# ScalarE's work in the attention stage in another order, with the block loads of queries and keys on ScalarE's queue

## The reference

```python
# A: neighbourhood attention, 4 heads of 64, a window of 8 x 16 tokens, and 512 context keys
s_lat = einsum('bhrqd,bhrikd->bhrqik', qg, kg) + bias      # -inf outside the window's columns
s_ctx = einsum('bhrqd,bhcd->bhrqc', qg, ck)
p = softmax(concatenate([s_lat, s_ctx], -1))
o = einsum('bhrqik,bhrikd->bhrqd', p_lat, vg) + einsum('bhrqc,bhcd->bhrqd', p_ctx, cv)
# D: chunked gated linear attention, both directions, a chunk of 64 tokens
o_intra = where(causal, q_dec @ k_inv, 0) @ v
state = decay * state + k_end @ v;  o_inter = q_dec @ state_at_start
```

## Time and profile before

| | us |
|---|---|
| median of 3 runs (lowest, highest) | 2887.41 (2885.74, 2889.26) |
| the profiled execution, its own time | 2884.65 |
| its span in the profile | 2882.9 |
| TensorE busy in the span | 2549.0 (88%) |
| ScalarE busy in the span | 971.1 (34%) |
| the attention stage: first scores to last scan output | 1660.3 to 2300.0 |

### The profile page before, as it was taken

One profiled execution on the slowest core, in us unless ns is written; L12 is line 12 of the kernel. 1 busy time (PEld: TensorE's weight loads), 2 busy tenths in 40 slices (PEclk: granted clock), 3 DMA queues, 4 the chain that ended last, 5 costly groups with the idle time before them and its releaser, 6 DMA issues. The chain is left out here.

```text
span 2882.9 us, 53072 instructions
## 1 busy us (share of the span) xinstructions
PE 2549.0 (88%) x18772; PEld 2050.2 (71%) x18772; DVE 1261.2 (44%) x2644; ACT 971.1 (34%) x1991; POOL 795.0 (28%) x1273
## 2 busy tenths in 40 slices
PE   3899999999999689999999577888888754899999
PEld 1688888888888578888888456666666622688887
DVE  2534434343443243333333145665666511666665
ACT  2444444444444332222222134544545411211110
POOL 2223333332333200000000134434444300444442
PEclk8999999999999889999999789999999978899999
DMA  7433333333333342222222488876777599666664
GB/s 286 139 108 113 116 121 102 117 120 106 115 115 104 112 168 100 95 95 95 95 95 88 108 175 182 180 163 157 167 164 167 122 282 245 219 205 206 206 205 143
DMA packets 286657, 425.19 MB, mean 147 GB/s; under 512 B 45045, under 2 KB 203029, under 8 KB 282795
## 3 DMA queue, kind: packets, MB, share of 16 engines
q1 hardware_dynamic: 273132, 389.25, 47.3%
q10 hardware_dynamic: 12831, 32.85, 3.3%
q0 software_dynamic: 544, 1.09, 0.2%
HBM read 288.74 MB, written 134.34 MB: 147 GB/s over the span
## 5 line engine op out<-in xcount | busy, mean ns | idle before, releaser
L258 PE MATMUL p_ps_m<-p_w_hi,p_h_hi 128*128 128x512 f32 x1904 | 771.1, 405 | 20.3 <-DVE p_h_lo L768 19.5
L259 PE MATMUL p_ps_m<-p_w_lo,p_h_hi 128*128 128x512 f32 x1904 | 750.7, 394 | 0.0
L260 PE MATMUL p_ps_m<-p_w_hi,p_h_lo 128*128 128x512 f32 x1904 | 749.1, 393 | 0.0
L258 PEld LDWEIGHTS p_ps_m<-p_w_hi,p_h_hi 128*128 128x128 f32 x1904 | 359.2, 189 | 99.5 <-issue 20.3
L260 PEld LDWEIGHTS p_ps_m<-p_w_hi,p_h_lo 128*128 128x128 f32 x1904 | 358.8, 188 | 80.5
L259 PEld LDWEIGHTS p_ps_m<-p_w_lo,p_h_hi 128*128 128x128 f32 x1904 | 359.5, 189 | 72.6
L258 PE MATMUL o_ps_y<-o_w_hi,o_y_hi 128*128 128x512 f32 x544 | 218.4, 401 | 9.7 <-DVE o_y_lo L1744 9.7
L259 PE MATMUL o_ps_y<-o_w_lo,o_y_hi 128*128 128x512 f32 x544 | 218.2, 401 | 0.0
L260 PE MATMUL o_ps_y<-o_w_hi,o_y_lo 128*128 128x512 f32 x544 | 214.5, 394 | 0.0
L1267 PE MATMUL a_ps_o<-a_v_win,a_p_t 128*64 128x64 f32 x2112 | 94.2, 230 | 100.8 <-DMA a_kv<-s_kv 39.8
L1267 PEld LDWEIGHTS a_ps_o<-a_v_win,a_p_t 128*64 128x64 f32 x2112 | 77.1, 140 | 138.6 <-issue 89.9
(11 more groups left out here) (202 smaller groups left out, 4469.7 us busy)
## 6 DMA issues: line engine op xcount, KB each, us to landing
p_xr<-in_x_sample SPq DMA_DIRECT2D x64, 512.0 KB, 3.9
p_xt<-in_x_sample_t SPq DMA_DIRECT2D x64, 512.0 KB, 4.6
a_scan<-s_scan SPq DMA_DIRECT2D x68, 258.0 KB, 5.6
s_scan<-p_w_raw SPq DMA_DIRECT2D x136, 128.0 KB, 2.4
a_kv<-s_kv SPq DMA_DIRECT2D x68, 256.0 KB, 6.3
a_v_win<-s_p SPq DMA_DIRECT2D x132, 128.0 KB
o_x<-in_x_sample SPq DMA_DIRECT2D x32, 512.0 KB, 4.9
out_y_sample<-o_y ACTq DMA_DIRECT2D x32, 512.0 KB, 4.4
```

The source lines that it names most:

```text
L258: pe.matmul(out, left_hi(k), right_hi(k), start=(k == 0), stop=False)
L259: pe.matmul(out, left_hi(k), right_lo(k), start=False, stop=False)
L260: last = pe.matmul(out, left_lo(k), right_hi(k), start=False, stop=(k == K8 - 1))
```

## The change

ScalarE's order within a unit is new. Before it was: copy of `v`, `copy_scan` at head 0, both exponentials of `v+2`, `scale_out` of `v`. Now it is: copy of `v`, the context exponential of `v+1`, `scale_out` of `v-1`, `copy_scan` at head 0, the window exponential of `v+2`. The loads of the next block's queries and keys leave SyncE's program and stand at the end of ScalarE's: three of queries at `c = 0`, head 0, three at `c = 0`, head 1, three of keys at `c = 1`, head 0, and three at `c = 2`, head 0. The very first block is still loaded by SyncE. TensorE, VectorE and GpSimd keep their programs, with all their waits.

```diff
@@ block.sync @@
-                if c < 3 and b is not None:
-                    after = next_tile(i + 3 - c, jb, b, 3, kb)
-                    if c == 0:
-                        if not isinstance(jb, int) or jb:
-                            sp.wait_ge(s_done, jb * 16)
-                            sp.wait_ge(q_set, jb * 8)
-                        load_queries(after[1], after[2], after[4])
-                    else:
-                        load_keys(after[1], after[2], after[4], (c - 1,))
@@ block.scalar @@
+        def unit_before(tile, h):
+            i, jb, b, c, kb = tile
+            return (tile, h - 1) if h else ((i - 1, jb, b, (c + 3) % 4, kb), NH - 1)
+        def unit_after(tile, h):
+            return (tile, h + 1) if h + 1 < NH else (next_tile(*tile), 0)
...
-            def exps(tile, h):
+            def exp_window(tile, h):
                 i, jb, b, c, kb = tile
                 p = h % 2
                 act.wait_ge(max_done, 4 * i + h + 1)
+                if b is not None:
+                    act.activation(s_sb[p][:, 0:N_WIN], s_sb[p][:, 0:N_WIN], ACT.Exp, bias=neg_m[:, p:p + 1], accum_out=sums[:, p, 0:1])
+            def exp_context(tile, h):
+                i, jb, b, c, kb = tile
+                p = h % 2
                 if b is None:
...
                 else:
-                    act.activation(s_sb[p][:, 0:N_WIN], s_sb[p][:, 0:N_WIN], ACT.Exp, bias=neg_m[:, p:p + 1], accum_out=sums[:, p, 0:1])
                     act.activation(s_sb[p][:, WIN_P:], ps_c[p][:, :], ACT.Exp, bias=neg_m[:, p:p + 1],
                                    accum_out=sums[:, p, 1:2]).then_inc(exp_done, 1)
...
                         act.activation(p_t[h % 2][:, WIN_P:], ps_t[1][:, :], ACT.Copy).then_inc(t1_sb, 1)
+                    next_one, next_h = unit_after(tile, h)
+                    if next_one:
+                        exp_context(next_one, next_h)
+                    if not isinstance(i, int) or v:
+                        scale_out(*unit_before(tile, h))
                     if h == 0 and (not isinstance(i, int) or i):
                         copy_scan(i - 1, 1 - c % 2)
                     ahead_tile, ahead_h = units_ahead(tile, h)
                     if ahead_tile:
-                        exps(ahead_tile, ahead_h)
-                    scale_out(tile, h)
+                        exp_window(ahead_tile, ahead_h)
+                    if b is not None and (c == 0 and h < 2 or c in (1, 2) and h == 0):
+                        after = next_tile(i + 3 - c, jb, b, 3, kb)
+                        if c == 0 and h == 0 and (not isinstance(jb, int) or jb):
+                            act.wait_ge(s_done, jb * 16)
+                            act.wait_ge(q_set, jb * 8)
+                        if c == 0:
+                            load_queries(after[1], after[2], after[4], (h,))
+                        else:
+                            load_keys(after[1], after[2], after[4], (c - 1,))
+            scale_out((LAST_STEP, BLOCKS, None, 1, 0), NH - 1)
```

More of the change, by code:

```diff
@@ L978, in load_keys, with load_queries @@
                     sp.dma_start(low_keys[kb][:, h::2, 0:n].bitcast(F32), io["qk_lo"][2:4, half, bass.ds(tok, n)].rearrange("p k t -> k p t")).then_inc(k_in[kb], 16)
-            def load_queries(jb, b, kb):
+            def load_queries(jb, b, kb, parts):
                 tok, n = (N_GRID, N_PROMPT) if b is None else (b * BQ, BQ)
-                for h in range(2):
+                for h in parts:
                     half = slice(h * HD, h * HD + HD)
@@ L1018, in load_bias @@
                                  io["btab"][e, :, :, first - r + WIN_H - 1:first - r + 2 * WIN_H - 1, :].rearrange("h q r x -> q h (r x)")).then_inc(bias_in[e], 16)
-            load_queries(0, BLOCKS - 1, 0)
+            load_queries(0, BLOCKS - 1, 0, range(2))
             load_keys(0, BLOCKS - 1, 0, range(2))
@@ L1038, in _ @@
                           *(n for d in DIRS for n in (tile_of(d, ni) * (HD * SCAN_W * 4), tile_of(d, ni) * (P * 2 * W_GRP * 4), tile_of(d, i - 1) * (P * W_GRP * 4))))
-                    if c == 0:
-                        ahead(sp, jb * 16, jb * 8, (b + 1) * (BQ * 4))
-                    elif c < 3:
-                        ahead(sp, key_at(b + 1) * (GRID_W * 4))
                 if nxt:
@@ L1166, in _, with load_keys, load_queries @@
             act.activation(ck_dup[:, :, :], ck_f[:, :, :], ACT.Copy).then_inc(ck_hi_done, 1)
-            def exps(tile, h):
+            def load_keys(jb, b, kb, parts):
+                tok, n = (N_GRID, N_PROMPT) if b is None else (key_at(b) * GRID_W, BK)
+                for h in parts:
+                    half = slice(h * HD, h * HD + HD)
+                    high = io["qk_hi"][2:4, half, bass.ds(tok, n)].rearrange("p k t -> k p t")
+                    for z in range(2):
+                        act.dma_start(k_dup[kb][z * HD:z * HD + HD, h::2, 0:n].bitcast(F32), high).then_inc(k_in[kb], 16)
+                    act.dma_start(low_keys[kb][:, h::2, 0:n].bitcast(F32), io["qk_lo"][2:4, half, bass.ds(tok, n)].rearrange("p k t -> k p t")).then_inc(k_in[kb], 16)
+            def load_queries(jb, b, kb, parts):
+                tok, n = (N_GRID, N_PROMPT) if b is None else (b * BQ, BQ)
+                for h in parts:
+                    half = slice(h * HD, h * HD + HD)
+                    high = io["qk_hi"][0:2, half, bass.ds(tok, n)].rearrange("p k t -> k p t")
+                    act.dma_start(q_blk[kb][0:HD, h::2, 0:n].bitcast(F32), high).then_inc(q_in[kb], 16)
+                    act.dma_start(low_q[kb][:, h::2, 0:n].bitcast(F32), high).then_inc(q_in[kb], 16)
+                    act.dma_start(q_blk[kb][HD:P, h::2, 0:n].bitcast(F32), io["qk_lo"][0:2, half, bass.ds(tok, n)].rearrange("p k t -> k p t")).then_inc(q_in[kb], 16)
+            def exp_window(tile, h):
                 i, jb, b, c, kb = tile
@@ L1196, in _ @@
             first = (0, 0, BLOCKS - 1, 0, 0)
-            exps(first, 0)
-            exps(first, 1)
+            exp_window(first, 0)
+            exp_context(first, 0)
+            exp_window(first, 1)
             for tile in query_tiles(act):
```

## The result

The changed kernel takes 2978.36 us (median of 4 runs, 2972.07 to 2982.49), against 2886.57 us (4 runs) before: a ratio of 1.0313, 95% interval 1.0295 to 1.0330. It is slower by 92 us, where 2923.5 was forecast with a range up to 2958. The profiled execution took 2979.53 us.

A forecast was written before the change was run, and what follows sets the result against it. TensorE was taken to bound most attention steps, with waits for `a_kv` and ScalarE's copy. 2884.65 + 48 (order) + 10 (loads on ScalarE) - 22 (SyncE) = 2920.7, plus 2.8 to the runs' median: 2923.5 us, range 2900 to 2958.

The forecast's parts named there:

- The direction: Whole kernel: slower 0.86, within 0.2% (5.8 us) of no change 0.05, faster 0.09.
- From `turn` to `values`: TensorE, attention tiles: 3.53 us instead of 2.67 at head 0, 2.74 at heads 1 to 3.
- The sum of +48: ScalarE's new order in the attention stage: +1.50 us per tile over 32 grid tiles, bounds 45 to 67.
- the 0.86 of that head: Head 0: `values` comes 3.53 us after `turn` instead of 2.67, since `copy_scan` now follows the later `scale_out`.
- The loads on ScalarE, +10: Block-load issues on ScalarE: 2.4 us at head 0, 8 at `c = 0`, head 1; between 3 and 35.
- rival 2: ScalarE's block-load issues take 1.2 us each, costing 49 in place of 10: 2962 us, chance 0.11.
- The late copy at `c = 0`, head 2: ScalarE: the load set at head 1 delays this copy by 0.96 us, 8 us together over 8 sets.
- What SyncE wins, -22: SyncE without block loads: TensorE's waits for `a_kv` shrink, 27 us won and 5 lost again.
- 3 to 5 us to spare: Next tile's scan data: landed at 18 to 20 us after `turn` of head 0, needed by TensorE at 22.7.
- Rival 1: Key transfers exceed the spare time, so the `a_kv` waits stay: 2946 to 2978 us, chance 0.17.
- Rivals 3 and 4: Rival 3: new order under 0.5 per tile, 2864, chance 0.08; rival 4: order at 0.5, about 2887, chance 0.06.

The follow-up runs named there:

- the fastest version of all: Against the kernel before: `scale_out` ahead of the copy, `copy_scan` right behind it, SyncE's stores behind its loads, block loads still on SyncE; 2871.13 us, ratio 0.9941.
- the run with the stores behind: Against the changed kernel: SyncE issues the loads of tile `i+1` first and stores tile `i-1` behind them; 2912.82 us, ratio 1.0093.

## Where the prediction was right and where it failed

**The direction was right** (slower, 0.86), the time was not: 2978.4 against 2923.5, 20 us above the range.

**From `turn` to `values`: right to 0.04 in the loop's tiles.** Forecast 3.53 at head 0 and 2.74 at heads 1 to 3, measured 3.53 and 2.70 to 2.71; undisturbed tiles 19.2 forecast, 18.9 to 19.1 measured where no issue stands in the way. The largest wait for ScalarE is the one for `scale_out`, but not the largest at `values`: that is the one for `a_kv` (79.0 against 73.6). **The sum of +48 was too large**: the order alone costs 31.6, with an interval of 24 to 37. A tile that waits for `a_kv` at head 0 doesn't pay the 0.86 of that head (11 tiles, some 9 us). The other 7 can be noise for the most part: the two profiled executions differ by 38.5 (2923.16 less 2884.65), which with the 9 makes the 48. That the cause is the place of `scale_out` behind the context exponential is shown for heads 1 to 3, where nothing else was moved when the cost went; at head 0 `copy_scan` was moved with it.

**The loads on ScalarE, +10: nearly nothing.** An issue takes 0.61, as forecast, so rival 2 (1.2 each) is out. But a set's first issue starts 0.13 to 0.30 after the window exponential has *started* (1908.77 and 1908.64), not behind its end, and so a set is over some 0.5 sooner than I had it. The late copy at `c = 0`, head 2, was forecast for all 8 blocks with 0.96; `values` is late there in 4 of the 8, by 0.35 to 0.60, 1.9 us in all. At head 1 there is a set in which one issue takes 1.93. The copy starts 0.12 after the last issue of that set ends, and `values` comes 0.6 late:

```profile
1953.71 1.93 ACTq L1179 DMA_DIRECT2D a_k_low<-s_qk_hi  x1
...
1955.73 0.61 ACTq L1180 DMA_DIRECT2D a_q_blk<-s_qk_lo  x1
1956.46 0.60 ACT L1225 ACTIVATE a_p_t<-a_ps_t 128x512 f32<-128x512 f32 x1 [3.01 <-PE a_ps_t L1280]
```

With the bytes taken away and the issues left, the time is 2915.3, not above that of the order alone. The issues cost more than a few us only where they were put at heads 2 and 3.

**What SyncE wins, -22: this is the step that failed, with its sign.** I counted SyncE's own time as what was short and took it as freed: values issued in 2.98 to 4.57, landing 6.3 later, 3 to 5 us to spare. The trace of before already speaks against it. In each of the 32 grid tiles SyncE waits for `scale_out` before its stores, 168.6 us in all. In the tile at 1907.78 the last load of queries is out at 1922.75, and the stores can start only at 1925.68. The block loads stood in time that SyncE had to wait anyway, so that taking them away moves no store and no load of a tile forward; in the changed kernel SyncE waits 294.1 us.

What the move did was the opposite of a gain: the waits for `a_kv` grew by 39.2 us, and their landing rose from 6.3 to 8.4. SyncE's issues did not get quicker either. The values' slow issue was there before (its rows from 1680 us on add up to some 143 us, twelve of them 5.4 to 8.0, more than the 4.57 that I took as the worst) and is there after (148); new is the slow load of scan data (53 us before, 87 after, twelve rows of 2.98 to 4.03). Slow issues of values alone need not cost: the fastest version of all has the most, some 171 us. Before, the block loads stood last on the common queue, behind what the next tile needs, and that order was worth more than the 4 us of issuing. Alone, the move costs 38.9.

**Rival 1** (the transfers' waits stay, 2946 to 2978, chance 0.17) was the right mechanism: three loads of keys or queries don't fit into the time to spare. That the measured time is at its very end is in part luck. The rival's sum has 58 us for the order and the issues, of which 31.6 and a few were measured, and it had the bytes' part too small: the waits not only stayed but doubled, and after the long ones the clock was lower. I had held against it that the keys are issued some 4 us ahead of the scan data; the runs with the loads two heads later show that this is what does the harm. The Trainium skill's rule ("DMA: Bandwidth & Descriptors", sections "Issuing engines are not separate DMA queues" and "Queues, rings and completion order") had stood against my gain: transfers of different engines share the same DMA engines, and a second issuing engine saves only issuing time. The runs agree: 2978.4 with the bytes, 2915.3 without, the issues the same.

**Rivals 3 and 4** need a new order at 0.5 per tile or less: it costs about 1 (31.6 over 32 tiles). The version with `scale_out` in front of the copy shows that such an order exists, and then 2885.7 comes out.

**The whole loss.** Of 91.8 us, 31.6 are the order, 38.9 the loads, and 21.3 more come only with both; by the intervals of the three runs this last figure is uncertain by some 12. Part of it is the clock. Matmul time per recorded matmul in the loop is 222.47/3688 = 60.3 ns; before it was 251.49/4320 = 58.2, with the loads alone 237.59/4035 = 58.9 and with the order alone 236.29/4084 = 57.9. At some 270 matmuls a tile (3688 in 13.6 tiles) and 32 tiles that is an estimated 18 us against before, 6 with the loads alone and -3 with the order alone, so some 15 of the 21. The rest would be that a later section and slower transfers come out of the same spare time; the run with the stores behind, which gives back 65.5, fits that, but the two were not separated. Open, too, is how the doubled waits divide in the changed kernel between slower issuing of scan data (as at 1916) and slower landing, which alone does it in the run with the loads alone, and why SyncE's issue slows.

## What to carry over

In these runs the program's order on one queue acted as a priority: the block loads behind the tile's own left them a landing of 6.3 us, and from a second queue ahead of them 8.4 to 10.7. The move can save only issuing time, and here the issuing engine waited anyway: read its waits before calling its time short. Before moving a load to another engine, compare when its bytes travel with when the urgent ones must land, and look for a place behind them at which its issues delay nobody; neither of the two places tried here was one. On an in-order engine, put the short step that another engine waits for (`scale_out`, 0.2 to 0.3 us) in front of the long ones, and ask of each instruction that is moved forward which signal it now stands in front of.

## What the runs showed of the hardware that I had not expected

- The issue of four loads of values by SyncE took 2.88 to 2.99 us in quiet stretches. Behind block loads it took 4.57 (before) and 5.85 (changed kernel) in the tiles shown, whichever queue these came from, and one load of scan data 0.53 or 2.98. In the run with the loads alone, though, it took 2.99 with queries on their way.
- A transfer's issue on ScalarE runs beside the exponential that stands ahead of it: it starts 0.13 to 0.30 us after that one's start. The next copy can still be held up by the rest of the set.
- A stall costs more than its length. After the wait of 4.97 us the granted clock is 0.50, and `scan_scores` took 1.97 instead of 1.15 us; over the loop the clock is 0.93 instead of 0.97.
